# A two-layer hybrid encoder on one core: inputs and mixed heads tile by tile in memory, and another order at the joints of its runs

## The reference

```
x = layer_norm(x, ln_in_g, ln_in_b)
for l in range(2):
    h = x @ w_in[l]           # columns: A q,k,v,gate; B latent q, latent kv, rotary key, gate; C q,k,v,gate
    a = window_attn(A)        # 8 heads, 2 kv heads, +-128 tokens, sink logit, relative bias
    b = mla(B)                # rms_norm of the latents, w_uq / w_uk / w_uv, rotary parts, 4 heads, dense
    c = neighborhood_attn(C)  # 4 heads on a grid 64 wide, learned 2-D bias
    o = concat(a * silu(gate_a), b * silu(gate_b), c * silu(gate_c)) @ w_out[l]
    x = layer_norm(alpha * x + o, ln_g[l], ln_b[l])
```

## Time and profile before

| | us |
|---|---|
| median of 3 runs (1889.70 to 1892.58) | 1891.92 |
| profiled execution | 1886.69 |
| its span | 1884.9 |
| mean granted clock of PE | 0.992 |

### The profile page before, as it was taken

One profiled execution on the slowest core, in us unless ns is written; L12 is line 12 of the kernel. 1 busy time (PEld: TensorE's weight loads), 2 busy tenths in 40 slices (PEclk: granted clock), 3 DMA queues, 4 the chain that ended last, 5 costly groups with the idle time before them and its releaser, 6 DMA issues.

```text
span 1884.9 us, 32231 instructions
## 1 busy us (share of the span) xinstructions
PE 1813.4 (96%) x12538; PEld 1473.1 (78%) x12538; DVE 945.2 (50%) x2058; ACT 774.6 (41%) x1668; POOL 437.1 (23%) x671
## 2 busy tenths in 40 slices
PE   5999998999999999999989999989999999999997
PEld 4787578889987665889978866988898766578897
DVE  5466665111424775554552466550133277665637
ACT  2355653221124666543232366441212266755510
POOL 2353412211111263001152223130111114600010
PEclk9999999999999999999999999999999999999999
DMA  5675432221124122004145452422212051200022
GB/s 188 181 252 161 109 121 86 75 67 46 46 67 114 33 64 79 1 1 146 43 133 175 144 136 68 158 77 67 67 46 67 23 146 39 82 23 1 23 79 90
DMA packets 148025, 166.13 MB, mean 88 GB/s; under 512 B 18290, under 2 KB 134386, under 8 KB 147364
## 3 DMA queue, kind: packets, MB, share of 16 engines
q1 hardware_dynamic: 145792, 157.64, 27.7%
q0 software_dynamic: 1152, 4.19, 0.6%
q10 hardware_dynamic: 932, 2.23, 0.3%
HBM read 141.96 MB, written 32.65 MB: 93 GB/s over the span
## 4 chain that ended last, share of the span: by engine, by line
PE 87%; DVE 7%; ACT 2%; issue 2%; DMA 1%; POOL 1%; SPq 0%; ACTq 0%; DVEq 0%
PE psum L632 63%; PE psum L757 8%; PE psum L727 8%; PE psum L709 6%; DVE nmax L1153 2%; PE psum L768 1%; DVE pt_sb L1177 1%; PE psum L642 1%; DVE qB_lo L1328 1%; DMA w_stage<-w_in 1%; DVE x_lo L1144 1%; ACT w_hi L928 0%; DVE qA L1129 0%; POOL w_lo L522 0%; PE psum L790 0%
## 5 line engine op out<-in xcount | busy, mean ns | idle before, releaser
L632 PE MATMUL psum<-w_hi,x_hi 128*128 128x256 f32 (+1 forms) x1344 | 379.8, 283 | 10.3 <-DVE x_lo L1351 6.7
L632 PE MATMUL psum<-w_hi,x_lo 128*128 128x256 f32 (+1 forms) x1344 | 379.4, 282 | 0.0
L632 PE MATMUL psum<-w_lo,x_hi 128*128 128x256 f32 (+1 forms) x1344 | 379.0, 282 | 0.0
L632 PE MATMUL psum<-x_hi,w_hi 128*128 128x512 f32 x816 | 327.5, 401 | 19.4 <-DVE x_lo L1144 9.7
L522 POOL TENSOR_TENSOR w_lo<-w_stage,w_hi 128x1024 fp32r<-128x1024 f32 (+1 forms) x82 | 167.6, 2053 | 732.6 <-ACT w_hi L928 732.5
L632 PE MATMUL psum<-x_lo,w_hi 128*128 128x512 f32 x816 | 325.8, 399 | 0.0
L632 PE MATMUL psum<-x_hi,w_lo 128*128 128x512 f32 x816 | 325.5, 399 | 0.0
L522 DVE TENSOR_TENSOR w_lo<-w_stage,w_hi 128x1024 fp32r<-128x1024 f32 (+1 forms) x78 | 137.2, 1775 | 330.8 <-ACT w_hi L928 330.4
L632 PEld LDWEIGHTS psum<-w_hi,x_hi 128*128 128x128 f32 x1344 | 256.5, 191 | 12.1 <-issue 8.2
L632 PEld LDWEIGHTS psum<-w_lo,x_hi 128*128 128x128 f32 x1344 | 255.0, 190 | 0.2
L632 PEld LDWEIGHTS psum<-w_hi,x_lo 128*128 128x128 f32 x1344 | 254.3, 189 | 0.0
(11 more groups left out here) (151 smaller groups left out, 2622.6 us busy)
## 6 DMA issues: line engine op xcount, KB each, us to landing
w_stage<-w_in SPq DMA_DIRECT2D x48, 512.0 KB, 4.2
w_stage<-w_in SPq DMA_DIRECT2D x88, 256.0 KB, 3.6
toep<-rpb_tile SPq DMA_DIRECT2D x12, 1152.0 KB, 16.2
rpb_tile<-rpb_col SPq DMA_DIRECT2D x48, 192.0 KB
hT<-y SPq DMA_DIRECT2D x18, 512.0 KB, 5.8
y<-hT SPq DMA_DIRECT2D x18, 512.0 KB, 2.7
w_stage<-w_out SPq DMA_DIRECT2D x32, 256.0 KB, 4.1
w_stage<-w_out SPq DMA_DIRECT2D x16, 512.0 KB, 5.0
```

The lines of the kernel that those rows point to most:

```text
L632: last = nc.tensor.matmul(out, w, x, start=(n == 0 and part != 1), stop=(n == len(pairs) - 1 and part != 0))
```

## The change

- `x_hi` and `x_lo` lie by tile: [128, 8 tiles, 8 chunks of rows, 128 tokens] instead of [128, 8 chunks, 1024 tokens]. The moving operand of a feature unit is now four runs of 128 floats. One buffer, `small`, holds the A bias and later B's small weights.
- Long runs: ck takes tokens 512 to 1023 (tiles 4 to 7) first; the x tiles are loaded and transposed in the order 4, 5, 6, 7, 0, 1, 2, 3; the earlier take_x of tile 7 at the run's start is gone. Output units 2 and 3 interleave with a distance of two tiles in runs that another follows.
- B: the value products go behind score 1 (long) or 2 (short), their copies on DVE behind the bound of that score.
- Mixed heads of tile 0: high part on ACT after the third last exponential, low part on DVE ahead of the last bound.
- The splits of the next run's first two units, and SP's stores and rpb spreads, change places with others. In run 0 the input norm's scale and bias come by broadcast DMA, and DVE does two splits that POOL did. In the last run each row is finished in its own step.

The core of the diff (row numbers of after differ by up to six):

```diff
-    return [(c, j) for c in range(SEQ_LEN[s] // 512) for j in range(1 if u == "ak" else 2)]
+    return [(c, j) for c in chunk_order(s, u) for j in range(1 if u == "ak" else 2)]
+
+
+def chunk_order(s, u):
+
+    n = SEQ_LEN[s] // 512
+    return range(n - 1, -1, -1) if u == "ck" else range(n)
...
+    NT, lag = NTILES[s], 2 if s + 1 < RUNS else 1
+    return [(u, t) for u in range(2) for t in range(NT)] + [x for t in range(NT + lag) for x in ((2, t), (3, t - lag))
+                                                            if 0 <= x[1] < NT]
...
+    return (4, 5, 6, 7, 0, 1, 2, 3) if s and NTILES[s] > 4 else tuple(range(NTILES[s]))
...
-        return {(1, 1): (4,), (1, 3): (5,), (2, 1): (6,)}.get((n, t), ())
+        return {(0, 3): (4,), (1, 1): (5,), (1, 3): (6,), (2, 1): (7,)}.get((n, t), ())
...
+            x_hi = sb("x_hi", [P, NTMAX, KC, P], F32R, st)
+            x_lo = sb("x_lo", [P, NTMAX, KC, P], F32R, st)
...
+            small = sb("small", [P, 2304], F32, st)
+            biasA = small[:, :].rearrange("p (t k n) -> p t k n", t=3, k=2)
+            wuq_sb = small[:, 0:2 * B_HEADS * BD].rearrange("p (c n) -> p c n", c=2)
+            wuk_sb, wuv_sb = small[:, 768:1024], small[:, 1024:1280]
+            gq0, gq1, gkv = (small[:, 1280 + i:1281 + i] for i in range(3))
+            rope_q = small[:, 1536:2048].rearrange("p (a b n) -> p a b n", a=2, b=4)
...
-            for key in [("bk", s, B_HEADS - 1, SEQ_LEN[s] // 512 - 1)] + \
-                    [("bv", s, t) for t in range(NT - 4, NT)]:
-                wait_read(pe, key)
+            wait_read(pe, ("bk", s, B_HEADS - 1, SEQ_LEN[s] // 512 - 1))
+
+        def b_value_rows(pe, s, NT, products):
+
+            for t in range(NT):
+                ps = wait_free(pe, ("bv", s, t))
+                products(("bv", s, t), ps[:, 0:256], None, [(ckvT[:, q_tile(t)], wuv_sb[:, :])])
...
-                    tok = slice(512 * c, 512 * (c + 1))
+                    tok = slice(4 * c, 4 * c + 4)
                     products((u, s, j, c), ps[:, :], None,
-                             [p for k in range(KC) for p in ((wh[:, k], x_hi[:, k, tok]), (wh[:, k], x_lo[:, k, tok]),
-                                                             (wl[:, k], x_hi[:, k, tok]))])
+                             [p for k in range(KC) for p in ((wh[:, k], x_hi[:, tok, k, :]), (wh[:, k], x_lo[:, tok, k, :]),
+                                                             (wl[:, k], x_hi[:, tok, k, :]))])
...
-                def rest_of_x(n):
+                def parts_of_x(n, c):
                     if n % 2 == 0:
-                        wait_parts(s, "xT", 2 * n)
-                    if s and n == 1:
-                        x_tiles(s, x_at_start(s))
+                        wait_parts(s, "xT", 4 * c)
+
                 if s == 0:
-                    pe.wait_ge(pre_row, 16 * 2)
-                    pe.wait_ge(pre_mem, 3)
-                    for n in range(4):
-                        nc.tensor.matmul(bank[n], one_row, gb_row[:, 512 * n:512 * n + 512], start=True, stop=True).then_inc(pre_wide, 1)
                     pe.wait_ge(ident_loaded, 16)
                     x_tiles(s, range(2))
...
+                        if kind == "V" and ph == "B" and i == 0:
+                            for t in range(NT - 4, NT):
+                                wait_read(pe, ("bv", s, t))
                         if kind == "S":
                             score(s, i, U[i])
+                            if ph == "B" and i == (1 if dense_wide(ph, s) else 2):
+                                b_value_rows(pe, s, NT, products)
...
-            for n, row in enumerate((ln_in_g, ln_in_b)):
-                act.dma_start(gb_row[:, DM * n:DM * n + DM], row.unsqueeze(0)).then_inc(pre_row, 16)
+            act.dma_start(pre_g, ln_in_g.unsqueeze(0).broadcast_to([P, DM])).then_inc(pre_gb, 16)
+            act.dma_start(pre_b, ln_in_b.unsqueeze(0).broadcast_to([P, DM])).then_inc(pre_bias, 16)
             act.dma_start(_all(ident), c_ident).then_inc(ident_loaded, 16)
-            act.wait_ge(pre_mem, 3)
+            act.wait_ge(pre_mem, 2)
...
+            def out_high(s, t):
+
+                wait_read(act, ("O", s, "B", t))
+                for h in range(2):
+                    k = slice(4 * h, 4 * h + 4)
+                    nc.scalar.activation(x_hi[:, t, k, :], gT[:, k, q_tile(t)], ACT.Copy).then_inc(o_hi_done, 1)
...
-                    for n, wide in enumerate((pre_g, pre_b)):
-                        act.wait_ge(pre_wide, 2 * n + 2)
-                        nc.scalar.activation(wide.rearrange("p (b n) -> p b n", b=2), psum[:, 2 * n:2 * n + 2, :],
-                                             ACT.Copy).then_inc(pre_gb, 1)
-                    norm_sqrt(pre_ln, 1)
-                    high_part(s, 0)
                     split_high(s, 0)
-                    high_part(s, 1)
-                    norm_sqrt(pre_ln, 2)
-                    high_part(s, 2)
-                    norm_sqrt(pre_ln, 3)
+                    for t in range(NT):
+                        high_part(s, t)
+                        if t + 1 < NT:
+                            norm_sqrt(pre_ln, t + 1)
                     split_high(s, 1)
-                    high_part(s, 3)
                     for t in range(NT):
                         act.dma_start(y_out[0][0, q_tile(t), :], pre_bufs[t]).then_inc(pre_yp, 16)
                 else:
-                    norm_last_rows(s - 1)
-                    for t in x_at_start(s):
-                        high_part(s, t)
+                    last = NTILES[s - 1] - 1
+                    norm_sqrt(layer_ln, ln_no[s - 1, last] - 1)
                     split_high(s, 1)
+                    for t in (last - 1, last):
+                        norm_rows(layer_ln, z_place(t), ln_no[s - 1, t] - 1)
...
+                        if ph == "B" and i == len(U) - 3:
+                            out_high(s, 0)
                 act.wait_ge(values_done, s + 1)
-                for t in range(NT):
-                    wait_read(act, ("O", s, "B", t))
-                    for h in range(2):
-                        k = slice(4 * h, 4 * h + 4)
-                        nc.scalar.activation(x_hi[:, k, q_tile(t)], gT[:, k, q_tile(t)], ACT.Copy).then_inc(o_hi_done, 1)
+                for t in range(1, NT):
+                    out_high(s, t)
...
+            def value_rows(s, NT):
+
+                for t in range(NT):
+                    key = ("bv", s, t)
+                    ps = wait_full(dve, key)
+                    nc.vector.tensor_copy(vB[:, t, :], ps[:, 0:256]).then_inc(free(key), 1)
...
+            def out_low(s, t):
+
+                for h in range(2):
+                    k = slice(4 * h, 4 * h + 4)
+                    dve.wait_ge(o_hi_done, 2 * ln_no[s, t] - 1 + h)
+                    nc.vector.tensor_tensor(x_lo[:, t, k, :], gT[:, k, q_tile(t)], x_hi[:, t, k, :].bitcast(F32),
+                                            ALU.subtract).then_inc(o_split, 1)
...
+                        if t == 1:
+                            split_low(dve, s, 0, 0)
+                            split_low(dve, s, 0, 1)
                         prompt_norm(t)
                     low_part(s, NT - 1)
                 else:
                     norm_coef((ln_stat, ln_sqrt, ln_coef), ln_no[s - 1, NTILES[s - 1] - 1] - 1)
                     tail_gain(s - 1, 2)
+                    split_low(dve, s, 1, 1)
                     tail_gain(s - 1, 1)
-                    if not x_at_start(s):
-                        split_low(dve, s, 1, 1)
                     tail_gain(s - 1, 0)
-                    for t in x_at_start(s):
-                        low_part(s, t)
-                    if x_at_start(s):
-                        split_low(dve, s, 1, 1)
...
                     if s == 0 and i == 0:
+                        split_low(dve, s, 1, 1)
...
                             bound_scores(s, i, U[i])
+                            if ph == "B" and i == (1 if dense_wide(ph, s) else 2):
+                                value_rows(s, NT)
...
+                        if ph == "B" and i == len(U) - 2:
+                            out_low(s, 0)
...
+                    if (n, t) == (3, NT - 3) and s + 1 < RUNS:
+                        split_low(dve, s + 1, 0, 1)
...
-                        if t and s == RUNS - 1:
+                        if s == RUNS - 1:
                             dve.wait_ge(lnp_loaded, 32 * RUNS)
-                            last_rows(t - 1, [slice(0, DM)])
+                            last_rows(t, [slice(0, DM)] if t < NT - 1 else [slice(0, 512), slice(512, DM)])
...
-                    if (n, t) == (2, NT - 1) and s + 1 < RUNS:
-                        split_low(dve, s + 1, 0, 1)
-                if s == RUNS - 1:
-                    last_rows(NT - 1, [slice(0, 512), slice(512, DM)])
...
                 for i in range(NI):
-                    if s == 0 or i > 1:
+                    if i > 1 or (s == 0 and i == 1):
```

(32 more changed lines are left out.)

82 lines of the change are left out of this document (25 added, 57 removed).

## The result

The changed kernel takes 1844.02 us (median of 4 runs, 1841.69 to 1846.45), the kernel before 1890.81 (4 runs, 1885.44 to 1892.58): a recorded ratio of 0.9765, 95% interval 0.9749 to 0.9780 (the two medians divided give 0.9753). The forecast was 1852, in a range of 1843 to 1868; the narrower 1846 to 1860, given for the case that the forecast is made for, lies just above the measured time. The profiled executions are 1886.69 and 1846.45, with spans of 1884.9 and 1844.7: 40.2 us apart, where the forecast's sum was 39.5.

What follows compares the result with a forecast made beforehand. PE was taken as the bound, busy 1813.4 of 1884.9 us, with its waits the thing to win. Terms summing to 39.5 took the profiled 1886.7 to 1847.2; plus 5.2 for the median gave 1852 us, range 1843 to 1868.

Steps and rivals of the forecast that it cites:

- Part 2: Both short-to-long switches: PE's 4.9 us waits for `x_lo` and the half clock behind them go; 13.5 us, floor 5.
- 0.3 of small waits: Short-to-long switches: with the lag between output units 2 and 3, some 0.3 us of small waits goes too.
- The 3.4: Short-to-long switches: half clock behind the two waits for `x_lo`, 2.1 and 1.3 us, goes.
- Part 3: Long-to-short switch: waits of 2.78 and 4.7 for weight loads behind row stores, and half clock, go; 9.4 us.
- The margin of 2 us for aq1: Long-to-short switch: aq1's load no longer follows three stores on SP, 6.7 us against the 4.7 wanted.
- rival B: Switches: weights still late, loads sharing DMA engines or DVE's split behind POOL's bias rows; 1864 us, chance 0.22.
- part 4: Four output starts: the 1.67 wait for `x_lo` goes at each, 0.55 to 0.7 comes back; 4.1 us, 1 to 6.7.
- part 5: Start of B: value products cover softmax waits, 1.3 per long run and 1.15 per short; 4.1 us, 1 to 5.
- Part 1: Start: broadcast scale and bias, first product at about 22.2, the 2.23 wait before aq1 gone; 6.7 us, 1 to 8.
- +0.6: Path to the first product: DVE's two splits add 2.56 us, tile 1's undisturbed normalisation saves 1.96.
- Parts 6 and 7: Tail: DVE's work on tile 6 one step earlier, 1.7 us; layout: moving operand in four runs, 0 us.
- The step from the profiled execution to the median: Whole kernel: 5.2 us added at the end because the old kernel's median, 1891.9, lies above its profiled 1886.7.

Runs made afterwards that it cites:

- The ck experiment: The changed kernel with ck of the long runs taking tokens 0 to 511 first again: 1854.67 us.
- the last one: The changed kernel with first-unit splits on POOL, second unit's split early, tile 2 transposed ahead, last bias row behind POOL's split: 1837.12 us.

## Why the prediction was right, point by point

The time came out 8 us under the forecast and 1 us above the lower end of the range. That the sum of the parts is off by only 0.7 us is in part luck: parts 1, 3 and 6 were together 2.1 too large, 4 and 5 together 2.9 too small. Undone one by one, the chunks of ck, the stores, tile 0, the values and the broadcast give back 12.4, 9.8, 5.6, 5.9 and at least 4.1: 37.8, beside the 40.2 by which the spans differ. The tail and the wait before aq1 in run 0 were not undone by a run of their own.

- **Part 2** (13.5 forecast, 13.5 measured) was right in place and cause, and in size but for two small things. The ck experiment gives 12.4 of it back by one edit: the last tile's `x_lo` still ends 4 us behind the last output product, only it is due a chunk later. The "0.3 of small waits" was none: PE's idle time in these stretches of the kernel before was 4.86 and 4.87, the one wait alone. The 0.3 came out by luck, in place of the 0.24 by which each wait costs more than its row. And 0.224 us for a product was read from a count that takes in matmuls cut by the window's ends; the starts from 954.38 on lie 0.234 apart. The 3.4 hardly changes, as the last window's 8 are 7 by the same reading.
- **Part 3** (9.4, 8.7) had the right cause: undoing the stores brings back 9.8. The margin of 2 us for aq1 was wrong. It counted SP's queue and not POOL's, where two bias rows stand ahead of the split: the outcome of rival B, weights late, through a queue that it had not named, at 0.47 us instead of 12. (The split of 2.64 that rival B cites stood behind a split on POOL, 318.22 to 320.62, and not behind a bias row.)
- **Parts 4 and 5** (8.2, 11.1) were sized too small. Undone one by one they give 5.6 and 5.9, where the forecast had 4.1 for each. For part 4 I priced each wait at its row, 1.67, where it costs 1.91, and took 0.55 to 0.7 back for DVE's two early pieces; PE waits only 0.54 (short) and 0.61 (long, where 0.17 was there before). 1.91 less these is 1.37 and 1.47, and 1.34 and 1.48 were measured. For part 5 I kept 0.2 of each wait, left out the same 0.24, and gave the value products no gain of their own; what makes up the rest of a short run's 1.43 these runs don't take apart.
- **Part 1** (6.7, 5.4) was right on the broadcast and on the first product (22.04 for 22.2). Up to ck's first matmul (44.28 for "near 44") it was right by luck: the second 1.67 in the first unit, which the sum took away, stayed, and the half clock that went from that unit (13 matmuls 0.21 us apart instead of 0.12, 1.2 us), which the sum did not have, made up for most of it. Behind it, two terms are missing: the half clock that went with the wait of 2.23 (8 matmuls in 3.48 us, 1.6 over full rate) and the one that came behind the new wait of 1.70 (2.6 us), which was in the sum with its own length only. The "+0.6" for the splits on DVE, right for the sum, does not say what the move is worth, as it compares them with POOL's as they lay before; with the weights loaded earlier POOL hardly collides, and the splits on DVE cost 2.3.
- **Parts 6 and 7** (1.7 and 0; 1.6 and 0) were right; the layout has a run of its own, the tail only the profile.
- **The step from the profiled execution to the median**, +5.2, failed. It took the distance of the kernel before over to the changed one, whose median is 2.4 below its profiled execution. Even for the kernel before it was a matter of three executions: the medians of later series, 7 to 13 executions each, are 1887.26 to 1888.81, 0.6 to 2.1 above the profiled one. 5.2 + 2.4 = 7.6 of the 8 us between 1852 and 1844 are this step; the sum itself is off by 0.7.

On rival B the rule of the Trainium skill that the prediction weighed (SBUF — State Buffer, "Who interferes with whom") was tried a second time by the splits on POOL. By it DVE's instruction at 15.18 waits for POOL's at most until 15.69 and then takes 1.28, 1.79 in all; the row has 1.59, so the trace agrees within 0.2. The rule says who waits; where it bites is decided by when the weights land.

## What to carry to other kernels

List the waits of the busiest engine, find for each what stands ahead of the late instruction in its own queue (a store on SP, a split on DVE, a bias row on POOL), and move that or make the late thing due later: five of six parts came out within 1.5 us of a sum of such rows, part 1 by errors that cancel. A wait's row is its lowest price: here 0.24 us more went with the one at the output start. A margin has to be worked out on every engine that takes part, and a cost that is read beside a collision holds only as long as the collision is there. Where a wait is added or taken away, price the slower clock behind it too, and don't carry the distance between one profiled execution and the median over to another kernel.

## What the runs showed of the hardware

The same instructions with the same wait ahead of them ran at different clocks. Run 0's ck began at half clock for about 14 matmuls in the first profile of the changed kernel, for 7 in the second, and for none with ck's chunks as before (25 matmuls in 5.62 us at 1.00), each behind a wait of 1.69 or 1.70 us. Of the eight profiles with that wait five show half clock behind it and three (ck's chunks, values, scale and bias as before) none; of the four profiles where it is 0.5 or 0.6 none does. From ck to ta the half clock costs 1.2 to 2.7 us (51.90 to 53.36 against 50.70). Of the four equal waits of 1.67 with tile 0 split late, one was followed by half clock. Over the executions time and mean granted clock go together: the kernel before took 1885.2 us at 0.993 and 1893.0 at 0.989, that with tile 0 split late 1847.8 at 0.998 and 1853.6 at 0.996; the four kernels without the wait of 1.7 in run 0 spread over only 0.3 to 0.7 us (1837.03 to 1837.30 for the last one), though two with it did too (1846.49 to 1847.32, 1847.75 to 1848.45). So a wait of 1.7 us costs its own length, some 0.2 at its ends, and now and then 1.2 to 2.7 us more. The levels of the run times are not this alone: the matmuls behind the first product that lie 0.21 us apart number 19 in the first profile of the changed kernel and 7 with the second unit's split earlier, another 1.1 us. What decides when the clock falls, and why even waits of 1.7 us do it, these runs don't settle.
